# A state-space branch: convolution, SiLUs and softplus inside the projection before it, tiles as a pipeline of 16 units

## What is computed

```python
proj = rms_norm(x) @ w_in                      # (1024, 5648)
z, xbc, dt_raw, ... = split(proj)              # 1024, 1536, 16 columns, and the other mixers'
xbc = silu(causal_depthwise_conv(xbc, conv_w, conv_b))      # 4 taps
xs, b_in, c_in = split(xbc)                    # 1024, 2 x 128, 2 x 128 columns
dt = softplus(dt_raw + dt_bias)                # 16 heads, in 2 groups of 8
a_cum = cumsum(dt * -exp(a_log))               # within chunks of 128 tokens
decay = exp(where(mask, a_cum[l] - a_cum[s], -inf))
y_diag = (c_in @ b_in.T) * decay @ (xs * dt)
states = b_in.T @ (exp(a_cum[-1] - a_cum) * xs * dt)        # then a scan over the 8 chunks
y_off = exp(a_cum) * (c_in @ previous_state)
y = y_diag + y_off + d_skip * xs
out = grouped_rms_norm(y * silu(z), norm_w, 2)
```

## Time and profile before

| | us |
|---|---|
| median of 3 runs | 3947.17 (3947.0 to 3952.96) |
| the profiled execution | 3942.68 |
| its span | 3940.9 |

### The profile page before, as it was taken

How to read it: one execution, slowest core, us unless ns; L and a number is a source line. 1 busy time by engine, 2 the same in 40 slices (tenths; PEclk the granted TensorE clock), 3 DMA queues, 4 the chain that set the end, 5 groups by cost and what they waited for, 6 DMA issues and landing times. The chain is left out here.

```text
span 3940.9 us, 53137 instructions
## 1 busy us (share of the span) xinstructions
PE 3162.8 (80%) x20733; PEld 2560.9 (65%) x20733; DVE 1812.8 (46%) x2419; ACT 1177.3 (30%) x1570; POOL 707.2 (18%) x389
## 2 busy tenths in 40 slices
PE   7999948886777992999997879999945637645699
PEld 6999937776443442888876339999944525534387
DVE  2005546664552324888885332000035755567422
ACT  2000024332550112777775212000023132222311
POOL 3223133320000002122220002223203201110000
PEclk9999969888788995999999899999966656766899
DMA  4223231101006215999997433222240030021321
GB/s 162 89 98 130 85 112 43 45 27 53 31 20 269 96 59 179 381 399 399 399 399 264 156 116 103 88 88 93 69 141 0 0 135 1 0 81 34 123 96 64
DMA packets 233186, 504.94 MB, mean 128 GB/s; under 512 B 34784, under 2 KB 95408, under 8 KB 231872
## 3 DMA queue, kind: packets, MB, share of 16 engines
q1 hardware_dynamic: 183888, 387.91, 27.1%
q10 hardware_dynamic: 39376, 80.81, 5.6%
q0 software_dynamic: 9776, 34.16, 2.3%
HBM read 397.72 MB, written 103.95 MB: 127 GB/s over the span
## 5 line engine op out<-in xcount | busy, mean ns | idle before, releaser
L358 PE MATMUL pin_psum<-pin_sb_w,pin_sb_hT 128*128 128x354 f32 (+1 forms) x5376 | 974.9, 343 | 19.5 <-DVE pin_sb_w L320 16.9
L358 PEld LDWEIGHTS pin_psum<-pin_sb_w,pin_sb_hT 128*128 128x128 f32 x5376 | 936.1, 189 | 55.1 <-DVE pin_sb_w L320 17.7
L3677 DVE TENSOR_TENSOR moe_sb_wlo<-moe_sb_raw,moe_sb_whi 128x2048 fp32r<-128x2048 f32 x192 | 438.0, 2287 | 91.8 <-ACT moe_sb_whi L3502 91.6
L3502 ACT ACTIVATE moe_sb_whi<-moe_sb_raw 128x2048 fp32r<-128x2048 f32 x192 | 367.4, 1916 | 133.9 <-DMA moe_sb_raw<-in_w_gate 50.0
L337 DVE TENSOR_SCALAR pin_sb_xt<-pin_psum,pin_sb_ss 128x353 f32<-128x353 f32 (+1 forms) x112 | 69.9, 627 | 720.6 <-PE pin_psum L358 720.4
L292 ACT ACTIVATE pin_sb_xt<-pin_psum,pin_sb_ss 128x353 f32<-128x353 f32 (+1 forms) x112 | 65.6, 592 | 798.6 <-PE pin_psum L358 798.0
L3745 PE MATMUL moe_psum<-moe_sb_whi,moe_sb_xhi 128*128 128x512 f32 x512 | 204.1, 399 | 15.7 <-DVE moe_sb_xlo L3681 15.6
L3745 PE MATMUL moe_psum<-moe_sb_whi,moe_sb_xlo 128*128 128x512 f32 x512 | 200.8, 392 | 0.0
L3745 PE MATMUL moe_psum<-moe_sb_wlo,moe_sb_xhi 128*128 128x512 f32 x512 | 200.7, 392 | 0.0
L249 POOL CAST pin_sb_w<-pin_sb_raw 128x2832 fp32r<-128x2832 f32 (+1 forms) x26 | 75.0, 2883 | 643.4 <-PE pin_psum L358 595.1
L251 POOL TENSOR_TENSOR pin_sb_w<-pin_sb_raw,pin_sb_w 128x2832 fp32r<-128x2832 f32 (+1 forms) x26 | 184.8, 7108 | 3.9 <-issue 0.2
(11 more groups left out here) (663 smaller groups left out, 5551.3 us busy)
## 6 DMA issues: line engine op xcount, KB each, us to landing
moe_sb_raw<-in_w_gate SPq DMA_DIRECT2D x64, 1024.0 KB
moe_sb_raw<-in_w_up SPq DMA_DIRECT2D x64, 1024.0 KB
moe_sb_raw<-in_w_down SPq DMA_DIRECT2D x64, 1024.0 KB, 13.1
pin_sb_raw<-in_w_in SPq DMA_DIRECT2D x16, 1412.0 KB
scratch_proj<-pin_sb_xt ACTq DMA_DIRECT2D x16, 1412.0 KB, 6.0
pin_sb_raw<-in_w_in SPq DMA_DIRECT2D x12, 1792.0 KB
scratch_proj<-pin_sb_xt ACTq DMA_DIRECT2D x12, 1792.0 KB, 6.3
scratch_ybuf<-moe_sb_yb ACTq DMA_DIRECT2D x32, 512.0 KB, 6.8
```

What stands on the lines that cost most here:

```text
L358: mm = te.matmul(ps[:, t, 0:cols], hT[a_part][:, k, t * P:(t + 1) * P], wt[b][w_part][:, k, :], start=(k == 0 and n == 0), stop=(k == KD - ...
L3502: s.activation(whi[q][:, :, :], raw[q][:, :, :], ACT.Copy).then_inc(hi, 1)
L3677: tt(wlo[q][:, :, :], raw[q][:, :, :], whi[q][:, :, :].bitcast(F32), ALU.subtract).then_inc(lo, 1)
```

## The change

The second projection gets an aside, `ConvAside`. When the columns of z (chunks 0 to 2) are stored, they are loaded back a tile at a time, gated by ScalarE in chunks 4 to 7 and stored again. When chunk 7 is stored, the convolution runs in 24 units (three parts of 512 columns, eight tiles), three in each of the chunks 8 to 15: SP loads four copies of the 128 x 512 tile, each shifted by one token (the projection now has three rows of zeros ahead of the tokens), VectorE multiplies them by tap weights that are spread over the partitions and adds them, ScalarE takes the SiLU, and SP stores the result in HBM. Two buffers of four tiles take turns. The softplus runs behind the evictions of chunks 9 and 10 and stays in SBUF as `dts`. Chunks 4 to 15 are written out instead of looped on SP, ScalarE and VectorE.

`ssd` keeps only the cumulative sums and the tiles. It loads its constants and then xbc and z tile by tile. The 16 units (tile, group) are written out as a pipeline; the groups share banks: two pairs take turns for the rows, and one each is for scores and transposes, offset, diagonal and state. The row matmuls use two copies of `sel` and `aT`, at partitions 0 and 32. ScalarE does the subtraction and clipping of rows with Relu and a bias; the identity times `xd` is added by TensorE. The norm runs behind units 10 to 15 in batches, and the last tile's after the loop.

```diff
@@ norm_project (pad rows; the row length need not divide by 128 now)
+        pad_p = P if n_cols % P == 0 else 16
+        zero = ph.sb("zero", [pad_p, n_cols // pad_p]) if pad_rows else None

@@ new class, called by norm_project as its aside
+class ConvAside:
+    written_out = 6
+    Z_FIRST, FIRST, PER = 4, 8, 3
+    PARTS = XBC // CONV_PART
+    UNITS = PARTS * NT
...
+    def fetch_z(self, sp, t):
+        if t >= 2:
+            sp.wait_ge(self.z_st, 16 * (t - 1))
+        sp.dma_start(self.zt[t % 2], self.z_rows(t)).then_inc(self.z_in[t % 2], 16)
+    def fetch(self, sp, k):
+        p, t = k // NT, k % NT
+        if k >= 2:
+            sp.wait_ge(self.conv_st, 16 * (k - 1))
+        col = COL_XBC + CONV_PART * p
+        for j in range(TAPS):
+            sp.dma_start(self.x[k % 2][j], self.proj[t * P + j:t * P + j + P, col:col + CONV_PART]).then_inc(self.x_in[k % 2], 16)
+    def keep(self, sp, k):
+        sp.wait_ge(self.silu_a, k + 1)
+        sp.dma_start(self.conv[...], self.x[k % 2][0]).then_inc(self.conv_st, 16)
+    def advance(self, sp, k):
+        if k == NT:
+            self.weights(sp, 2)
+        self.keep(sp, k)
+        if k + 2 < self.UNITS:
+            self.fetch(sp, k + 2)
+    def sync(self, sp, c):
...
+        if c == 7:
+            self.fetch_z(sp, 0)
+            self.fetch_z(sp, 1)
+        if 8 <= c <= 10:
+            for t in (2 * c - 16, 2 * c - 15):
+                self.keep_z(sp, t)
+                self.fetch_z(sp, t + 2)
+        if c == 11:
...
+            self.fetch(sp, 0)
+            self.fetch(sp, 1)
+            sp.dma_start(self.dts[:, 0, :]..., dt, ...).then_inc(self.dt_in, 16)
+            for k in range(2):
+                self.advance(sp, k)
+        if 12 <= c <= 15:
+            for k in range(3 * c - 34, 3 * c - 31):
+                self.advance(sp, k)
+    def sync_end(self, sp):
+        for k in range(14, self.UNITS):
+            self.advance(sp, k)
+        sp.wait_ge(self.conv_st, 16 * self.UNITS)
+    def scalar(self, s, c, t):
+        if self.Z_FIRST <= c < self.FIRST and t in (2, 6):
+            i = 2 * (c - self.Z_FIRST) + t // 4
+            s.wait_ge(self.z_in[i % 2], 16 * (i // 2 + 1))
+            s.activation(self.zt[i % 2], self.zt[i % 2], ACT.Silu).then_inc(self.z_gated, 1)
+        if c >= self.FIRST:
+            k = self.PER * (c - self.FIRST)
+            if t == 4:
+                self.silu(s, k)
+            if t == 6:
+                self.silu(s, k + 1)
+                self.silu(s, k + 2)
...
+    def convolve(self, v, k):
+        v.wait_ge(self.x_in[k % 2], 16 * TAPS * (k // 2 + 1))
+        for j in range(TAPS):
+            v.tensor_tensor(x[j], x[j], w[:, j, :], ALU.mult)
+        v.drain()
+        v.tensor_tensor(x[0], x[0], x[1], ALU.add)
+        v.tensor_tensor(x[2], x[2], x[3], ALU.add)
+        v.drain()
+        v.tensor_tensor(x[0], x[0], w[:, TAPS, :], ALU.add)
+        v.drain()
+        v.tensor_tensor(x[0], x[0], x[2], ALU.add).then_inc(self.conv_d, 1)
+    def vector(self, v, c, t):
+        if t < 7:
+            self.convolve(v, self.PER * (c - self.FIRST) + t // 2)
+        elif c == self.FIRST + 1:
+            self.dt_biased(v)
+        elif c == self.FIRST + 2:
+            self.dt_softplus(v)

@@ ssd, GpSimd, for each tile
+                tt(xdd[b][:, :, :], xs, bcast(ddt[:, t, :], SP_), ALU.mult)
+                tt(xdt[b][:, :, :], xs, bcast(dts[:, 0, SH * t:SH * (t + 1)], SP_), ALU.mult)
+                tt(xd[b][:, :, :], xs, bcast(skip[:, :], SP_), ALU.mult).then_inc(prepared, 1)

@@ ssd, ScalarE, for each unit
+            def decay(u):
+                s.wait_ge(row_p, u + 1)
...
+                for i in range(HG):
+                    ins = s.activation(seg[q][:, seg_slot(i), :], row_block(u, i), ACT.Relu, bias=acum[:, t, h:h + 1], scale=-1.0)
+                s.activation(seg[q][:, :, :], seg[q][:, :, :], ACT.Exp, scale=-1.0).then_inc(decay_a, 1)

@@ ssd, VectorE, for each unit
+            def join(u):
+                ve.wait_ge(off_p, u + 1)
+                tt(y[q], h64(OFF), bcast(eac[:, t, heads(q)], SP_), ALU.mult).then_inc(off_d, 1)
+                if t + 1 < NT:
+                    tt(S[:, heads(q), :], S[:, heads(q), :], bcast(cdec[...], SP_), ALU.mult)
+                    ve.wait_ge(state_p, u + 1)
+                    tt(S[:, heads(q), :], S[:, heads(q), :], h64(STATE), ALU.add).then_inc(state_d, 1)
+                ve.wait_ge(diag_p, u + 1)
+                tt(y[q], y[q], h64(DIAG), ALU.add).then_inc(diag_d, 1)
+                ve.wait_ge(z_in[t], 16)
+                tt(z[:, t, cols(q)], y[q]..., z[:, t, cols(q)], ALU.mult).then_inc(gated, 1)
+            for u, (t, q) in enumerate(units):
+                if q == 1 and t + 1 < NT:
+                    score(t + 1)
+                if u + 1 < UNITS:
+                    mask(u + 1)
+                join(u)
...

@@ ssd, TensorE, for each unit
+            def rows(u):
+                    te.matmul(row_block(u, i), sel[lane:lane + SH, h * P:(h + 1) * P], aT[lane:lane + SH, t * P:(t + 1) * P], ...)
+            def sums(u):
+                te.matmul(ps[:, OFF, :], BCt[b][:, 2 + q, :], S[:, heads(q), :]..., ...).then_inc(off_p, 1)
+                te.wait_ge(prepared, t + 1)
...
+                    te.matmul(ps[:, STATE, :], xbc[:, t, SW + q * SN:SW + (q + 1) * SN], xdd[b]..., ...).then_inc(state_p, 1)
+                te.wait_ge(masked, u + 1)
+                if u:
+                    te.wait_ge(diag_d, u)
+                for i in range(HG):
+                    te.matmul(o, seg[q][:, seg_slot(i), :], xdt[b][:, h, :], start=True, stop=False)
+                    mm = te.matmul(o, ident, xd[b][:, h, :], start=False, stop=True)
+            for u, (t, q) in enumerate(units):
+                if t + 1 < NT:
+                    turn(t + 1) if q == 0 else score(t + 1)
+                sums(u)
+                if u + 2 < UNITS:
+                    rows(u + 2)
```

More of the change, by code:

```diff
@@ L2294, in put_back @@
-            def put_back(k):
-                s.wait_ge(back.sem, back.done(k))
-                s.activation(xbc[:, :, k * P:(k + 1) * P], blocks(ps, 4 + 2 * (k % 2), 8), ACT.Copy).then_inc(put.sem, 1)
-            for c in (held, silu, put):
-                c.begin(s)
-            s.drain()
-            s.wait_ge(zeroed, 1)
-            for k in range(NX + 2):
-                if k < NX:
-                    hold(k)
-                if 1 <= k <= NX:
-                    gate(k - 1)
-                if 2 <= k < NB + 2:
-                    put_back(k - 2)
@@ new lines, in square, with roots @@
+            def square(u):
+                t, q = units[u]
+                s.drain()
+                s.wait_ge(gated, u + 1)
+                s.activation(junk[:, :], z[:, t, cols(q)], ACT.Square, accum_out=ss[:, 0, u:u + 1]).then_inc(squared, 1)
+            def roots(tiles):
+                part = slice(SG * tiles[0], SG * (tiles[-1] + 1))
+                s.wait_ge(mean, tiles[-1] + 1)
+                s.activation(ss[:, 2, part], ss[:, 1, part], ACT.Sqrt).then_inc(root, len(tiles))
+            hold(0)
@@ L2502 @@
+            turn(0)
+            score(0)
+            te.wait_ge(sel_in, 16)
+            te.wait_ge(aT_d, 1)
+            rows(0)
+            rows(1)
+            for u, (t, q) in enumerate(units):
+                if t + 1 < NT:
+                    turn(t + 1) if q == 0 else score(t + 1)
+                sums(u)
+                if u + 2 < UNITS:
+                    rows(u + 2)
 HH, HD = 4, 128
```

562 lines of the change are left out of this document (290 added, 272 removed).

## The result

The changed kernel takes 3759.82 us in the median of four runs (3755.67 to 3764.86) against 3947.09 for the kernel before (3941.74 to 3952.96), a ratio of 0.952 (95% interval 0.951 to 0.9535). The forecast was 3795 with a range of 3762 to 3846: right in sign and in the bound that it named, but 35 us too pessimistic and 2 us outside its range. The result lies next to rival 1 (3764), whose mechanism for the row matmuls is the one that the runs show. The profiled execution took 3761.07 us with a span of 3759.3; the clock's mean is 0.89 where it was 0.87.

What follows compares the result with a forecast made beforehand. No engine was full in the state-space phase: engines took turns at a mixed clock. Profiled execution 3942.7, less 170 there, plus 18 in the projection, gives 3791; the runs' median lies 4.5 higher: 3795 us, range 3762 to 3846.

Steps and rivals of the forecast that it cites:

- rival 1: State-space loop: row matmuls run in pairs, halving their 2.05 us; unit 7.6 us, projection loses 8, total 3764; chance 0.16.
- start of the phase to the first diagonal sum: State-space phase: masks, cumulative product, transposes, first rows and sums until the first diagonal sum ends, at about 26 us.
- the other 15 units: State-space loop: TensorE sets the pace at 9.0 us per unit, 15 units 135 us, less 7 for the last.
- tail: End of the state-space phase: gate, square, root with table load, two norms, store and barrier, 10 us.
- projection: Second projection: hidden convolution, SiLUs and softplus cost 4 to 10 us stall and a 12 us later store, together 18.
- eight row matmuls at 2.05 us: State-space loop on TensorE: each unit's eight row matmuls at full clock take 2.05 us, from the trace before.
- an engine which is nearly always busy keeps the full clock: State-space loop: TensorE, over 90% busy at 9.0 us per unit, would have a clock over 0.9.
- Waits already met: State-space loop on TensorE: eight groups behind waits already met add some 0.5 us per unit, an estimate.
- Offset and state: State-space loop on TensorE: offset and state sums take 1.02 us each, 2.0 us per unit.
- The seven taken off: State-space loop: 7 us less because the last two units make no rows and the last tile no state.
- Rival 2: Projection becomes VectorE-bound: chunks 9 to 15 overshoot by 5 us each, 47 us lost, total 3824; chance 0.15.
- Rival 4: Projection: serial hand-over through HBM, 17.7 us per convolution unit, total 3964; slower than before from 16.8; chance 0.03.

Runs made afterwards that it cites:

- one-lane run: Changed kernel with all row matmuls reading partitions 0 to 15 while the banks still alternate; ratio 0.9595 to the kernel before, phase 160.3 us.
- run with 48 rows: Changed kernel with only the first partition group filled and each row matmul reading 48 partitions, the added rows zero; ratio 0.9564 to the kernel before, phase 147.2 us.
- empty aside: Changed kernel with convolution, SiLUs and softplus left out; ratio 0.9507 to the kernel before, projection 540.9 us.
- run with more work: Changed kernel with four more two-input 128x512 VectorE instructions in each of the 24 convolution units; ratio 0.9621 to the kernel before, projection 586.4 us.
- serial hand-over: Changed kernel fetching each convolution unit only when the one before is stored; ratio 0.9883 to the kernel before, projection 678.5 us.
- clipping on VectorE: Changed kernel with subtraction and clipping of the rows back on VectorE, ScalarE keeping the Exp; ratio 0.9588 to the kernel before, phase 170.9 us.

## Why the prediction was wrong by 35 us

The profile forecast stood at 3791 and the profiled execution at 3761.

| step | forecast | measured |
|---|---|---|
| start of the phase to the first diagonal sum | 26 | 21.0 |
| the other 15 units | 15 x 9.0 - 7 = 128 | 105.2 |
| tail | 10 | 12.0 |
| projection | +18 | +6.3 |
| unchanged phases | 0 | +7.5 |

The units are the largest gap, 22.8 us, and the projection the second, 11.7. No single one of these gaps was enough to leave the range: all but the tail and the unchanged phases erred to the same side.

**The step that failed: eight row matmuls at 2.05 us.** The forecast took the duration of the old loop, in which all of them read the same partitions, for a loop in which they alternate between two groups of partitions and two banks. They take 1.16, and the one-lane run, in which the banks still alternate, brings the 2.05 back. The price stands twice in the sum: at the start "rows of unit 0 and 1, 3.8 each" is in fact one row of 32 records:

```profile
2911.98 3.79 PE L2609 MATMUL ssd_psum<-ssd_sb_aT,ssd_sb_sel 16*128 16x128 f32 x32
```

3.8 us for both units instead of 7.6. That does not explain the start, though: on one lane the same row takes 5.53, with 48 partitions 4.97, and the first diagonal sum still ends 21.0 and 21.1 us into the phase. Which term of the 26 was too long stays open.

How much the row matmuls are worth in the whole sum shows where the old price stands at the full clock, in the run with 48 rows: a unit of 7.85 and a phase of 147.2, where the forecast had 9.0 and 164. So 8.5 to 8.9 of the 26 us of the phase are the row matmuls, and the other 17 are the small terms below and the start. The one-lane run's 160.3 lies near the 164 by luck: 13.1 us of it are the half-rate stretches, which the forecast did not have. Its sentence that an engine which is nearly always busy keeps the full clock failed there, with 96 of 96 us busy at 0.88.

The Trainium skill ("TensorE: Matmul & The Clock Gate", Part 3: Packing small matmuls) states that matmuls on different row groups run at the same time. By that rule the forecast had 1.1, and the trace agrees with 1.16. The forecast gave that rule 0.16 because no row of the kernel before showed it; but nothing in the trace spoke against it either, and the argument used against it, that the diagonal matmuls are bound otherwise, has nothing to do with the row matmuls.

**Three small terms on the same side.** Waits already met were put at 0.5 us a unit and cost nothing; no row bears a bracket. Offset and state were put at the 1.02 shown for one alone, but behind each other they start 0.86 apart, 0.3 less. The diagonal took 3.6 (2962.55 to 2966.16), not 3.8. Then 8.8 was rounded up to 9.0. Together these are 1.2 us a unit, more than the 0.9 of the rows, and with those they are about the whole distance from 9.0 to 7.0. An interval from the start of an instruction to that of the next one is the price of a stream; the shown duration is that of one in isolation.

**The seven taken off.** The forecast took 7 us off for the last units, which have no rows or state. The trace has 105.2 for 15 units, as much as 15 full ones: what these units lack, the ones before them lose again, behind ScalarE's table loads for the square root and VectorE's norms. Behind the last unit the norms of four tiles are left (two instructions each, 1.4 us a tile), three more than the forecast had, and the tail is 12 instead of 10.

**The projection: right model, load overestimated.** The 18 us were the second step that failed. The aside costs 6.0 us (empty aside), in two places: the stall of 2.24 (forecast 4 to 10) and an end 3.6 us later (forecast 12). The forecast let unit 0 run into GpSimd's split; in the trace it ends at 2669.9, 1.1 us ahead of it, and unit 1 takes the split alone (11.10 us). Unit 2's taps had by then arrived, so it followed at 2685.20 without a round. In the two chunks that followed VectorE freed the bank of tile 7 some 7 us ahead of TensorE, instead of 2, and that of tile 5 some 5 ahead. And at the end, with no split left, units come 6.1 to 8.4 us apart, so unit 23 starts 2.4 us ahead of the last matmul's end instead of far behind. The run with more work shows that the margin is real and narrow: 8.1 us more a chunk cost 39.5 in all. Rival 2 named the right danger, and its price of 5 us a chunk is what the added work cost (39.5 over eight chunks).

**The 2 us outside the range.** Rival 1 was worked out at 3764 with 7.6 a unit and its own spread was cut off at 3762. A rival that is a better case deserves a lower end of its own. Without the 0.5 for met waits its unit is 8.3 - 1.0 = 7.3 instead of 7.6, and its own mechanism also halves the rows at the start: 15 x 0.3 + 3.8 = 8 us, an end of 3756. (The 7.6 itself does not follow from its sum, 8.8 less 1.0, which is 7.8.) That the result fell within 4 us of rival 1 is in part luck: its phase was 4.7 us too long and its projection 1.7, and the 7.5 us of the unchanged phases made up for them. Rival 4's break-even has a slip as well: with the 12 us behind the last chunk it is (250 + 158)/24 = 17.0 us a unit, not 16.8; nothing hangs on it.

**Right.** The bound moved to TensorE, in the profiled execution at full clock; the other engines wait for it; the Relus cost 2.2 with no table loads around them; GpSimd's products lie beside TensorE, and they stretch VectorE's instructions with two SBUF inputs; the loads of x and z hide; the unchanged phases behind differ by 1.4 us.

## What to carry to other kernels

Before pricing a matmul of few rows by a duration of the trace, look at which partitions it and its neighbours read: on two groups of partitions and two banks the pair costs little more than one (1.16 us for eight against 2.05), and the clock may hang on it too. Before crediting a term with a whole miss, put its old price back at the same clock: here that left 17 of 26 us to other terms. Price a stream by start-to-start intervals and give the best case a lower end without surcharges. When a bound is removed, ask at once which wait stands first in each in-order queue: here 0.9 us less of TensorE a unit brought 0.26, and 0.43 once the mask stood behind work that was ready.

## What the runs showed of the hardware

- TensorE's granted clock fell although it was never idle: with the eight row matmuls of 16 partitions one behind the other it was 0.88 over 96 us, full in some units and halved from shortly behind the row matmuls of the others; with 48 partitions and the same durations it was 1.00. In the changed kernel, where two groups of 16 run side by side, it was 1.00 over the units in one profile and 0.97 over 105 us in the other; the runs with the empty aside, more work in the aside and the serial hand-over, whose state-space phase has the same order of work, have 0.98, 0.97 and 0.97. Elsewhere (clipping on VectorE) it fell to 0.82 with TensorE busy for 124 of 133 us; why there was not tested.
- Two groups of partitions side by side: eight matmuls of 16 x 128 in full fp32 took 1.16 us at the full clock when they alternated between partitions 0 and 32 and between two banks, and 2.05 when only the banks alternated. Whether one bank would do as well was not tested.
- Beside GpSimd VectorE stands still with more than the two-input operations that the forecast counted: a scalar operation of 128x128 from SBUF to SBUF, 0.23 us elsewhere in the same softplus, took 6.16 beside the split of 6.16 us. Operations of 128x512 that read PSUM kept 0.68 to 0.69 us in the kernels with the changed loop. The Trainium skill ("SBUF — State Buffer", SBUF: two separate sides) says that the two engines share a port pair which one of them holds for a whole instruction; the four products that took 11.10 instead of 2.50 us agree with that.
